# An encoder layer with split-precision matmuls: first weights in two halves, zero matmuls at the start, and another order in attention and around the second norm

## The reference

```python
def encoder_layer(x, ...):                      # 512 tokens and 256 tokens, model width 1024
    h = rms_norm(x, norm1_g)
    z = h @ w_in                                # columns: pool 512 | q 8x64 | k 2x64 | v 2x64
    mix = concat(pool_mixer(zp, pool_w, pool_scale),      # 4 groups of 128: windowed means, 128x128 map
                 gqa_attention(zq, zk, zv, ...))          # per-head norm, rotary turn, softmax over keys
    x = x + mix @ w_out
    return x + peer_ffn(rms_norm(x, norm2_g), peer_wq, peer_subkeys, peer_u, peer_v)

def peer_ffn(xn, wq, subkeys, u, v):            # 8 heads, 2 x 128 keys, top 16, 16384 experts
    q = xn @ wq;  s = q . subkeys;  e, g = top 16 of the sums of two top 16s, and their softmax
    a = gelu(xn . u[e]) * g
    return sum over chosen experts of a * v[e]
```

## Time and profile before

| | us |
|---|---|
| median of three runs | 2006.67 |
| the three runs | 2014.74, 2006.67, 2004.99 |
| profiled execution | 2015.25 |
| its span, first to last instruction | 2013.3 |
| DVE busy in it | 1625.2 |
| ACT busy in it | 986.8 |
| POOL busy in it | 796.7 |

### The profile page before, as it was taken

How to read it: one execution, slowest core, us unless ns; L and a number is a source line. 1 busy time by engine, 2 the same in 40 slices (tenths; PEclk the granted TensorE clock), 3 DMA queues, 4 the chain that set the end, 5 groups by cost and what they waited for, 6 DMA issues and landing times.

```text
span 2013.3 us, 28964 instructions
## 1 busy us (share of the span) xinstructions
PE 1963.7 (98%) x10186; PEld 1672.3 (83%) x10186; DVE 1625.2 (81%) x3120; ACT 986.8 (49%) x2052; POOL 796.7 (40%) x604
## 2 busy tenths in 40 slices
PE   7999998999899999999999999999999999999999
PEld 7977897988788888888888888778888888888887
DVE  3556425688999999999987777799989998998897
ACT  5255424323578778787878784322232223222321
POOL 0444200001333333323345555565545555554552
PEclk9988899999999999999999999999999999999999
DMA  6110212124888888989899999999999999999996
GB/s 261 42 35 1 111 46 105 68 96 141 278 306 290 295 306 304 305 295 334 296 317 377 372 379 411 391 388 395 389 406 393 406 404 395 404 379 407 403 391 226
DMA packets 203075, 581.23 MB, mean 289 GB/s; under 512 B 19904, under 2 KB 57152, under 8 KB 200640
## 3 DMA queue, kind: packets, MB, share of 16 engines
q0 software_dynamic: 73728, 268.47, 36.5%
q1 hardware_dynamic: 77616, 243.97, 31.9%
q10 hardware_dynamic: 51600, 67.12, 9.2%
HBM read 505.03 MB, written 74.45 MB: 288 GB/s over the span
## 4 chain that ended last, share of the span: by engine, by line
PE 64%; DVE 4%; ACT 3%; DMA 3%; issue 1%; ACTq 0%; POOL 0%; SPq 0%; DVEq 0%
PE ps L319 20%; PE ps L320 20%; PE ps L321 20%; PE ps L1404 5%; DMA g_dram<-arena_a 1%; ACT arena_a L658 1%; DMA arena_b<-g_dram 1%; ACT arena_a L662 1%; DMA ring_b<-in_u_rows,expert_ids 0%; DVE ring_a L1104 0%; DVE ring_b L1104 0%; DVE w_lo L1014 0%; ACT arena_b L704 0%; DVE arena_b L996 0%; DVE arena_b L993 0%
## 5 line engine op out<-in xcount | busy, mean ns | idle before, releaser
L319 PE MATMUL ps<-v_hi_slots,w_lo 128*128 128x512 f32 x1024 | 399.3, 390 | 6.3 <-DVE w_lo L1142 6.3
L321 PE MATMUL ps<-v_hi_slots,w_lo 128*128 128x512 f32 x1024 | 399.0, 390 | 0.0
L319 PE MATMUL ps<-feat_hi,w_hi 128*128 128x512 f32 (+1 forms) x936 | 360.4, 385 | 0.0
L320 PE MATMUL ps<-feat_lo,w_hi 128*128 128x512 f32 (+1 forms) x936 | 351.7, 376 | 0.0
L321 PE MATMUL ps<-feat_hi,w_lo 128*128 128x512 f32 (+1 forms) x936 | 351.4, 375 | 0.0
L685 ACT ACTIVATE w_lo<-arena_a 128x512 fp32r<-128x512 f32 x128 | 81.3, 635 | 501.6 <-PE ps L321 459.1
L797 POOL DMA_INDIRECT ring_a<-in_u_rows,expert_ids x86 | 116.6, 1356 | 338.1 <-DVE ring_a L1104 176.1
L319 PEld LDWEIGHTS ps<-v_hi_slots,w_lo 128*128 128x128 f32 x1024 | 192.7, 188 | 47.2 <-issue 5.6
L321 PEld LDWEIGHTS ps<-v_hi_slots,w_lo 128*128 128x128 f32 x1024 | 192.6, 188 | 40.1
L321 PEld LDWEIGHTS ps<-feat_hi,w_lo 128*128 128x128 f32 x936 | 176.4, 188 | 32.1
L319 PEld LDWEIGHTS ps<-feat_hi,w_hi 128*128 128x128 f32 x936 | 177.0, 189 | 28.4
(11 more groups left out here) (207 smaller groups left out, 4495.2 us busy)
## 6 DMA issues: line engine op xcount, KB each, us to landing
arena_a<-in_v SPq DMA_DIRECT2D x128, 512.0 KB
w_raw<-in_uT SPq DMA_DIRECT2D x85, 512.0 KB
g_dram<-arena_a ACTq DMA_DIRECT2D x64, 512.0 KB
gel_dram<-arena_b ACTq DMA_DIRECT2D x120, 256.0 KB
w_raw<-gel_dram SPq DMA_DIRECT2D x120, 256.0 KB
arena_a<-in_uT SPq DMA_DIRECT2D x43, 512.0 KB
w_raw<-in_w_all SPq DMA_DIRECT2D x17, 1024.0 KB, 5.6
arena_b<-g_dram SPq DMA_DIRECT2D x32, 512.0 KB
```

Source lines behind the costliest of these rows:

```text
L319: nc.tensor.matmul(out, lh, rh, start=first, stop=False)
L320: nc.tensor.matmul(out, lh, rl, start=False, stop=False)
L321: return nc.tensor.matmul(out, ll, rh, start=False, stop=last)
```

## The change

The first chunk's weights are loaded and split in two halves of four feature tiles, the first half ahead of everything else, and TensorE multiplies zeros nine times before the first product:

```diff
+            sp.dma_start(Wr[:, 0, 0:4, :], io["w_all"][0, :, 0:4, :]).then_inc(w_half, 16)
             sp.dma_start(vecs[:, :], io["vecs"]).then_inc(vec_in, 16)
-            load_w(0, 0)
-            for k in range(KD):
+            for k in range(2):
+                load_xt(k)
+            sp.dma_start(Wr[:, 0, 4:8, :], io["w_all"][0, :, 4:8, :]).then_inc(w_in[0], 16)
+            for k in range(2, KD):
                 load_xt(k)
...
-            pe.wait_ge(w_lo, 1)
+            pe.wait_ge(zero_v, 2)
+            for i in range(9):
+                last = mm(ps[:, 7, :], KV_[:, 2 * TOK:2 * TOK + P], KV_[:, 2 * TOK:2 * TOK + 512], start=True, stop=True)
+            last.then_inc(warm, 1)
+            pe.wait_ge(w_half_lo, 1)
             for k in range(KD):
+                if k == 4:
+                    pe.wait_ge(w_lo, 1)
                 pe.wait_ge(ft_lo, k + 1)
```

DVE turns the odd tiles of q and k, POOL the even ones. The transposes of q and k are interleaved with the pool windows and maps; the fourth group's windows and maps run inside the first pass. All of q is split into high and low parts as it is evicted (into `FTh[:, r - 1]` and `FTl[:, r - 1]`), so `take_pair` goes. The units of a pass are ordered by `groups`, and TensorE's passes are written out instead of looped:

```diff
-        units = [(q, hh, t + i) for q, (t0, n) in enumerate(SEQ_TILES) for t in range(0, n, 2)
-                 for hh in range(2) for i in range(2)]
+        groups = [(0, 0, 0), (1, 0, 0), (0, 0, 1), (0, 2, 0), (0, 2, 1), (1, 0, 1)]
+        units = [(q, hh, t + i) for q, t, hh in groups for i in range(2)]
...
+            pe.wait_ge(small_in, 16 * len(smalls))
+            pe.wait_ge(rope_ok, TT // 2)
+            pe.wait_ge(rope_dve, TT // 2)
+            flip_qk(0)
+            pe.wait_ge(z_ev, 6 + 30)
+            windows(0)
+            flip_qk(1)
             windows(1)
             group_map(0)
+            flip_qk(2)
             windows(2)
             group_map(1)
-            windows(3)
+            flip_qk(3)
             group_map(2)
-            flip_qk(0)
-            group_map(3)
-            for r in range(1, 5):
-                flip_qk(r)
+            flip_qk(4)
...
             def pair(j, first=False):
-                pe.wait_ge(q_lo, j + 1)
                 for u in range(3):
+                    if first and u == 2:
+                        pe.wait_ge(mix_lo, 6)
                     scores(j, u)
+                if first:
+                    windows(3)
                 for u in range(NU):
                     if u + 3 < NU:
                         scores(j, u + 3)
+                    if first and u == 0:
+                        group_map(3)
+                    if first and u == 5:
+                        pe.wait_ge(mix_lo, 8)
+                        pe.wait_ge(v_parts, 2)
...
-            with pe.Fori(1, 4) as j:
+            for j in range(1, 4):
                 pair(j)
```

```diff
+            for i, t in enumerate(y_tiles):
+                if i == 5:
+                    flipped(0)
+                    flipped(1)
...
+            for i in range(8, 16):
+                flipped(i)
+            act.dma_start(y_dram.rearrange("t p d -> p t d"), y[:, 0:DT, :]).then_inc(y_out, 16)
             w_split_hi(10)
...
+                    if h == 0 and n == 2:
+                        pe.wait_ge(y_ev, 6 + 24)
+                        for i in range(8, 16):
+                            flip_y(i)
```

The dots start later, and the first gates are loaded two slabs earlier in SP's list:

```diff
-    return 8 * min(e + 1, 82) // 5 + 13 * max(e - 81, 0) // 5
+    return 5 * max(min(e - 3, 78), 0) // 3 + 13 * max(e - 81, 0) // 5
...
-                if e == v_first + 9:
+                if e == v_first + 7:
                     sp.wait_ge(g_out[1], 16 * 4 * (NBLK // 2))
                     sp.wait_ge(gts_ok, 2)
                     for piece in range(4):
                         load_gates(0, piece)
                 if e + 6 < NK:
                     sp.wait_ge(u_lo, e + 4)
                     load_u(e + 6)
```

More of the change, by code:

```diff
@@ L480, in _ @@
             w_split_hi(1)
+            act.wait_ge(warm, 1)
             for t in range(TT):
@@ L570, in pair @@
                         pt_out(j - 1, NU + u - 3)
-                    if u in (0, 5) and not first:
+                    if u in (2, 5) and not first:
                         o_out(j - 1, u // 5)
@@ L862, in _ @@
                               rs10[:, 10 * t:10 * t + 10].unsqueeze(2).to_broadcast([P, 10, 64]), ALU.mult))
-                tt(zn[:, t % 2, :], zn[:, t % 2, :], gqk, ALU.mult).then_inc(zn_ok, 1)
+                ins = tt(zn[:, t % 2, :], zn[:, t % 2, :], gqk, ALU.mult)
+                if t % 2 == 0:
+                    ins.then_inc(zn_ok, 1)
+                    continue
+                steps.step(ins)
+                ta, tb, turns = rope_views(t, rt_dve)
+                for a, c, b, s, op, dst in turns:
+                    steps.did(tt(ta, a, c, ALU.mult))
+                    steps.step(tt(tb, b, s, ALU.mult))
+                    steps.step(tt(dst, ta, tb, op))
+                dve.sem_inc(rope_dve, 1)
             w_split_lo(5)
@@ L911, in pair @@
                     nc.vector.reciprocal(rrec[:, u:u + 1], rsum[:, u:u + 1]).then_inc(sum_inv, 1)
+                    if first and u == 2:
+                        mix_rest(3)
                     if u >= 3:
@@ L1337, in _, with flip_y @@
             pe.wait_ge(o_lo, 2 + 8)
+            def flip_y(i):
+                k = i % 8
+                if i == 0:
+                    pe.wait_ge(y_ev, 6 + 20)
+                elif i == 8:
+                    pe.wait_ge(xs_act, 2)
+                    pe.wait_ge(xs_dve, 2)
+                if i >= 4:
+                    pe.wait_ge(xn_lo, i - 3)
+                for m, t in enumerate((4, 5) if i < 8 else (0, 1, 2, 3)):
+                    src = yt(t) if i < 8 else xs[:, t, :]
+                    last = nc.tensor.transpose(ps[:, 4 + i % 4, m * P:(m + 1) * P], src[:, k * P:(k + 1) * P],
+                                               ident[:, :])
+                last.then_inc(xn_tr, 1)
             with pe.Fori(0, N_WOUT) as c:
                 pe.wait_ge(w_lo, c + 6)
-                for t in range(TT):
-                    pe.wait_ge(y_ev, c * 6 + (t + 1))
+                for i, t in enumerate(y_tiles):
+                    pe.wait_ge(y_ev, c * 6 + (i + 1))
                     for k in range(KD):
@@ L1376, in _ @@
                     p = n % 2
-                    pe.wait_ge(xn_lo, 8 if n < 2 else 16)
+                    if h == 0 and n == 2:
+                        pe.wait_ge(y_ev, 6 + 24)
+                        for i in range(8, 16):
+                            flip_y(i)
+                    if h == 0 and n < 2:
+                        pe.wait_ge(y_ev, 6 + 22)
+                    if n >= 2:
+                        pe.wait_ge(xn_lo, 16)
                     if h:
```

252 lines of the change are left out of this document (136 added, 116 removed).

## The result

| | before | after |
|---|---|---|
| median of 12 runs, us | 2012.87 | 2001.58 |
| shortest and longest of them | 2003.34, 2018.15 | 1997.73, 2012.33 |
| profiled execution | 2015.25 | 2007.67 |
| its span | 2013.3 | 2005.8 |

The ratio of after to before is 0.9948, with a 95% interval of 0.9929 to 0.9967: the change makes the kernel about 0.5% faster. The forecast was 1990 us in a range of 1972 to 2005; the measured time lies in the range, and the gain, 11.3 us between these medians and 10.1 between the means further down, is about half of the 19.6 us that the sum gave.

A forecast was written before the change was run, and what follows sets the result against it. TensorE, busy 98% of the span, was taken as the bound, through its waits, low clock and moved instructions. Seven terms sum to -19.6 from 2015.25, giving 1995.7; less 6 us for shorter runs, 1990 us, range 1972 to 2005.

The forecast's parts named there:

- 1 head: Kernel start: split weights and zero matmuls start products earlier, but second columns still wait for 1/rms; 0 us, -1.7 to +0.5.
- 2, 3, 5: Pool mixing and rotary turns (-4 us), attention pass boundaries (-3.6), and second norm (-1).
- 4 clock in attention: Attention: earlier, longer value runs leave 17 us at 1.2 GHz instead of 41.2, price 8.4 instead of 20.6; -12 us.
- 6 dots: First slabs: three dots leave the chain ahead of tile 0's gates, shortening TensorE's pause; -6.5 us, -3.4 to -9.
- 7 gates: Seam between long loops: gates loaded two slabs earlier hold back u loads, stopping slab 126 for 7 us; +7.5 us.
- Terms 2 and 3: Before attention, shared rotation and moved windows, -4 us; at three pass boundaries, q split beforehand, -3.6 us.
- Term 5: Second norm: small tiles projected while the norm is taken, -1 us; y's store might hold TensorE 1 to 2 us.
- allowance of 6 us: Taken off the 1995.7 us sum because shorter runs were assumed to have fewer low-clock passes; gives 1990.
- no hold-up at slab 126: Rival at the seam: stores finish before SP arrives, so the gates term becomes -2; 1980 us, chance 0.20.
- the clock never falls: Rival in attention: full clock throughout, clock term -20.6; 1981 us, chance 0.10.
- attention stays slow: Rival: evenly spread value matmuls never raise the clock, attention at 1.2 GHz from its first pass; 2045 us, chance 0.08.
- falls at every pass as now: Rival in attention: the clock falls as in the kernel before, clock term 0; 2002 us, chance 0.15.

The follow-up runs named there:

- Filled kernels: Kernels given extra products, whose results are overwritten, in some of the places where TensorE waited; measured means run from 1984.55 to 2001.55 us.
- old head: Late gates with three extra products per pass, given the earlier kernel's head (first weights in one transfer, no zero matmuls): mean 1986.88 us.
- filled kernel: Late gates plus three overwritten 512-column products ahead of the third score tile of passes 2 to 4: mean 1987.72 us.
- before, filled: Kernel before, plus four overwritten products ahead of every pass's third score tile and four ahead of the first tile of passes 2 to 4: mean 2001.55 us.
- changed, filled: Changed kernel, gates still loaded at slab 120, plus three overwritten products at the start of passes 2 to 4: mean 1997.42 us.
- old dots: Dots of the kernel before (8 per 5 slabs from the start): on the changed kernel 2009.26 us, on the filled kernel 1993.77 us.
- late gates: Changed kernel with the second loop's first gates loaded at slab 122 again instead of 120: mean 1994.49 us.
- all waits filled: Late gates with three extra products per pass, plus overwritten products in five more TensorE waits: mean 1986.99 us.

## Why the prediction was off

Filled kernels give each term a price without the clock's spread; the second line is what the others leave, so the sum closes by itself. The clock's own price is the difference that filling makes; filling made a pass of the kernel before 0.7 us longer (23.87 from filling to filling, against 23.17), 2.8 us in four passes by estimate, which is added there.

| term | forecast | measured | from |
|---|---|---|---|
| 1 head | 0 | +0.8 ± 0.7 | old head on the filled kernel |
| 2, 3, 5 | -8.6 | -5.8 ± 1.7 | what is left of before, filled, to changed, filled |
| 4 clock in attention | -12 | -8.8 ± 1.7 | (2003.05 - 1997.42) - (2013.15 - 2001.55 + 2.8) |
| 6 dots | -6.5 | -6.0 ± 0.5 | old dots on the filled kernel |
| 7 gates | +7.5 | +9.7 ± 0.7 | late gates on the filled kernel |
| sum | -19.6 | -10.1 | means of all runs |

The 2.8 us decide how much goes to the second row and how much to the third: without them the two would be -8.6 and -6.0. Two other counts stand closer to the table. Read from single profiles, as told below, terms 2, 3 and 5 come to -2.0, -1.6 and -1.9, together -5.5. And over the 63 runs of the kernel before whose clock is on record, each microsecond at 1.2 GHz (2 x (1 - clock) x span) goes with 0.43 us of span; the changed kernel has 40.7 of them in the mean of its runs and the kernel before 57.6, which makes 7 us by estimate, for the whole program.

**Term 4 is the step that failed most.** It took 41.2 us at 1.2 GHz from one profile, halved them, and charged the kernel before 20.6 us. The runs say 14.4. Two things are in that. First, work at the low clock does not take twice as long. In the fall shown above (late gates) 128x256 products follow each other at 0.213 us, in nine steps from the first to the last row here, against 0.12 at the full clock:

```profile
151.47 0.42 PE L334 MATMUL ps<-w_lo,keys_values 128*128 128x256 f32 x1
...
153.39 0.41 PE L334 MATMUL ps<-w_lo,keys_values 128*128 128x256 f32 x1
```

So a microsecond at 1.2 GHz costs 0.44 us and not 0.5. That fits the third pass, which had 17.1 us at 1.2 GHz and was 30.59 - 23.17 = 7.4 us longer than the second, not 8.6, with the same waits at its start. Second, how long the falls last is not a property of the order: the changed kernel had 13.6 us at 1.2 GHz in attention in one profile and 27 in another, and 19 of 75 runs of the kernel before were in a group some 12 us shorter. One profile and three runs, two of them from that smaller group, don't carry a number for it.

For the changed kernel the guess of 8.4 was too high as well (5.6), and its picture was wrong in three ways. The first pass, expected to fall, keeps the clock in all seven unfilled profiles that have the change: in its first wait TensorE now has the fourth group's windows, which fits what filling does but was not tested by itself. The later passes were expected to fall once in three; in the five profiles with the new order and without filling the clock fell at 14 of 15 starts of passes 2 to 4, but 10 of the 14 falls lasted 3.4 us, two 6.8, one 23.9 and one 27.3. And twelve value matmuls early in a pass were to keep the clock; the old order does as well. Why most falls are so short stays open; the waits at a pass's start are shorter than before (0.71 us in place of 1.4 to 1.8), but with the old order of units they are 0.90 us and the clock fell at one of six starts.

**Terms 2 and 3** were sized too high. The fifth score tile, forecast at 125.1, begins at 128.55, so 26.0 us behind the last eviction of z instead of 28.0: -2.0 where -4 was forecast.

```profile
128.55 0.50 PE L333 MATMUL ps<-keys_values,feat_hi 64*128 64x512 f32 x1
```

TensorE now waits 1.76 us for DVE's share of the rotation, of which the prediction saw only that POOL's part goes. DVE's instruction takes 1.06 us while POOL rotates too, and 0.49 us when POOL has ended (at 102.71):

```profile
99.84 1.06 DVE L901 TENSOR_TENSOR arena_a<-arena_a 128x320 f32<-128x320 f32 x1
...
103.09 0.49 DVE L901 TENSOR_TENSOR arena_a<-arena_a 128x320 f32<-128x320 f32 x1
```
```profile
99.53 1.01 POOL L783 TENSOR_TENSOR arena_b<-arena_b 128x320 f32<-128x320 f32 x1
...
101.72 0.99 POOL L785 TENSOR_TENSOR arena_a<-arena_b 128x320 f32<-128x320 f32 x1
```

The Trainium skill, SBUF — State Buffer, section "SBUF: two separate sides", says that DVE and GpSimd lock a pair of ports against each other when DVE reads two operands. These rows agree with it. A pass's start was to get 1.2 us shorter; a pass at the full clock got 0.54 shorter (23.17 to 22.63), three of them 1.6. With the old order of the units it would have been 1.09 (22.08): the new order takes half of it back.

**Term 5** has no run of its own. In the profiles the stretch from the output product to tile 0's pause is 1.9 us shorter (forecast 1), with the wait for the last feature of the large tiles as its largest (1.98 us) and 3.4 us at 1.2 GHz behind it. The feared wait on y's store falls on ACT, which stands 3.85 us for it, and not on TensorE, which has no wait there. The store took 6.6 us where 7 was forecast, though 2 MB at the 400 GB/s named would be 5.2:

```profile
314.90:318.40 3.50, 3.22 (x8) 2.54 (x9) 2.52 (x2) 1.10 (x2) 0.00 (x0) 0.51 1.02 408
```
```profile
319.85 0.38 ACT L638 ACTIVATE arena_a<-ps 128x256 f32<-128x256 f32 x1 [3.85 <-DMA y_dram<-arena_a]
```

**Term 1** had its mechanism right: the second columns still wait for 1/rms, and the restart behind a pause is slow. The pause (4.1 us) was forecast at 4.7, and the 3.4 us at 1.2 GHz behind it cost about what was charged (1.5 us by estimate, for 1.7). But the chain to the first eviction moved later by 0.6 us, since the second weights land later and ACT splits them only at 18.25 instead of 17.73, and that was put at no change.

**Term 6** was right in size and place, but the clock still fell behind the shorter pause, for 3.4 us instead of 6.8. **Term 7** was right in mechanism: the loads of u behind the gates, slab 126 stopped for 7.5 us where 7 was forecast. It was 2.2 us too small: in the profile of the changed kernel, filled, the start of the second loop waits twice more (3.4 and 3.6 us), where the prediction had the old 1.1 us wait vanish. With that one line as before, the kernel runs in 1994.5 (median 1991.84).

**The base.** The allowance of 6 us for fewer low passes in shorter runs came out by luck: the median of after lies 6.1 below its profiled execution, but 1.5 in the second set of runs of the same kernel. By its own rule, terms 4 and 7 at either bound, the range would begin at 1970 and not at 1972; nothing hangs on it. Of the rivals, that there is no hold-up at slab 126, that the clock never falls and that attention stays slow are refuted; "falls at every pass as now" (2002 forecast) is nearest in time, though by another way: the clock does fall at nearly every later pass, but mostly for 3.4 us, so term 4 is not 0, and the other terms gave less.

## What to carry to other kernels

The time at the low clock in one profile is one draw of several: look at the granted clock of several runs before pricing it, and test it by filling the short waits with products whose result is overwritten; here 0.9 us of such work in each of three passes saved 5.6 us of the changed kernel, and 2.3 us in each of three and 1.2 in the first saved 11.6 of the one before. When a load is moved ahead in a queue, price every instruction that is now behind its wait; one line moved by two slabs cost 9.7 us, nearly all that the other parts gave apart from the clock (11.0). Compare small parts of a change on a version whose runs agree within 3 us, not on one that spreads over 15.

## What the runs showed of the hardware

A wait of TensorE of 0.55 us at the start of a pass was enough to be followed by 1.2 GHz, for 3.4 us or for up to 27 us (late gates, second pass: 2 x 0.41 x 33.4), and the same wait in another run was not (changed kernel, second pass, 1.00). The Trainium skill, TensorE: Matmul & The Clock Gate, section "A second HAM failure mode: psum-queue depth-cycling", tells of short idling between groups of matmuls that makes the clock go up and down. The runs agree: filling the idle time ended it.

The length of a wait does not decide by itself. The one for DVE's rotation, 1.74 to 1.78 us in twelve profiles, was never followed by 1.2 GHz, nor was the one of 3.06 us with all waits filled.

Zero matmuls did not make sure of the full clock for the products behind them. Of ten profiles with the nine zeros, three have the full pace of 0.12 us for a 128x256 product from the first real one on. In three the clock was low for 3.4 us from 9.3, 10.1 or 10.2 us on, at the end of a wait of 1.9 to 2.9 us or up to 1.3 us behind it. In four the products began at 0.21 us each and took 2.8 to 4.1 us to come to 0.12. The row is of late gates, filled:

```profile
10.20:13.60 3.40, 3.40 (x19) 3.40 (x18) 3.08 (x4) 3.31 (x4) 0.00 (x0) 0.50 1.03 410
```

And a low clock cost little where TensorE then waits for weights: raising the granted clock from 0.995 to 0.999 of the run was worth 0.7 ± 0.6 us.
